# Order of the expert row gathers on GpSimd: four rows of U and four of V in turn, in place of one and one

## The reference

```python
def peer_ffn(h, w_q, sub_keys, u_tab, v_tab):
    q = (hf @ w_q).reshape(n_tok, PEER_HEADS, 2, PEER_HALF)
    half_scores = jnp.einsum('thpd,hpnd->thpn', q, sub_keys)
    s_top, i_top = lax.top_k(half_scores, PEER_TOPK)
    ...
    best, pos = lax.top_k(cand, PEER_TOPK)
    expert_idx = jnp.take_along_axis(cand_idx, pos, axis=-1)
    gates = jax.nn.softmax(best, axis=-1)
    def block(args):
        xb, ib, gb = args
        act = jnp.einsum('td,thkd->thk', xb, u_tab[ib])
        w = gb * jax.nn.gelu(act, approximate=False)
        return jnp.einsum('thk,thkd->td', w, v_tab[ib])
```

## Time and profile before

| | us |
|---|---|
| median of 3 runs | 2479.94 (2478.25 to 2479.95) |
| profiled execution, its own time | 2479.11 |
| its span, first to last instruction | 2477.4 |
| TensorE busy | 1984.5 (80%) |
| DVE busy | 1280.2 (52%) |
| GpSimd busy | 552.6 (22%) |
| ACT busy | 264.5 (11%) |
| moved by DMA | 793.18 MB, mean 320 GB/s |

### The profile page before, as it was taken

One profiled execution on the slowest core, in us unless ns is written; L12 is line 12 of the kernel. 1 busy time (PEld: TensorE's weight loads), 2 busy tenths in 40 slices (PEclk: granted clock), 3 DMA queues, 4 the chain that ended last, 5 costly groups with the idle time before them and its releaser, 6 DMA issues.

```text
span 2477.4 us, 19344 instructions
## 1 busy us (share of the span) xinstructions
PE 1984.5 (80%) x7000; PEld 1284.3 (52%) x7000; DVE 1280.2 (52%) x1633; ACT 264.5 (11%) x521; POOL 552.6 (22%) x551
## 2 busy tenths in 40 slices
PE   0399999998999999979677777777776777777777
PEld 0388888887888888868432222222222222222223
DVE  8634577775222122168865555565564444444443
ACT  0011112221000000020110101001011100010001
POOL 1000000000000000002454333334344333333341
PEclk9999999999999999999899999999998999999999
DMA  9868676553344336328899999999997999999996
GB/s 398 370 248 335 257 306 271 221 225 164 136 143 162 135 107 264 121 110 336 328 415 421 422 422 422 422 422 422 422 421 323 422 422 422 421 422 422 422 422 263
DMA packets 92379, 793.18 MB, mean 320 GB/s; under 512 B 10657, under 2 KB 10657, under 8 KB 11313
## 3 DMA queue, kind: packets, MB, share of 16 engines
q0 software_dynamic: 78512, 606.14, 59.0%
q1 hardware_dynamic: 13824, 186.55, 19.4%
q10 hardware_dynamic: 2, 0.02, 0.0%
HBM read 790.57 MB, written 2.10 MB: 320 GB/s over the span
## 4 chain that ended last, share of the span: by engine, by line
DMA 40%; PE 40%; DVE 13%; issue 4%; POOL 1%; ACT 1%; DVEq 0%; POOLq 0%; ACTq 0%; SPq 0%
DMA arena<-expert_u,expert 37%; PE ps L529 27%; PE ps L537 9%; DVE arena L1004 6%; DMA arena<-ada 2%; PE ps L690 2%; DMA arena<-expert_v,expert 1%; DVE mod_rows L731 1%; DVE buf_b L739 1%; POOL arena L361 1%; DVE work L827 1%; DVE work L824 1%; PE ps L545 1%; PE ps L644 0%; PE ps L677 0%
## 5 line engine op out<-in xcount | busy, mean ns | idle before, releaser
L690 PE MATMUL ps<-arena,work 128*128 128x512 f32 x1520 | 703.6, 608 | 254.1 <-DMA arena<-expert_v,expert 234.8
L1004 DVE CUSTOM_DVE_ANT_0 arena<-arena,buf_b 128x2048 f32<-128x2048 f32 x256 | 585.7, 2292 | 525.7 <-DMA arena<-expert_u,expert 524.6
L690 PEld LDWEIGHTS ps<-arena,work 128*128 128x128 f32 x1520 | 278.5, 192 | 678.1 <-issue 509.1
L361 POOL DMA_INDIRECT arena<-expert_u,expert x256 | 267.9, 1046 | 1220.2 <-DVE work L1004 695.3
L529 PE MATMUL ps<-buf_a,arena 128*128 128x256 f32 x2304 | 507.7, 382 | 10.9 <-DVE arena L845 5.2
L529 PEld LDWEIGHTS ps<-buf_a,arena 128*128 128x128 f32 x2304 | 440.8, 192 | 74.8 <-issue 14.7
L690 PE MATMUL ps<-mod_rows,work 128*128 128x512 f32 x504 | 230.6, 601 | 75.2 <-DMA mod_rows<-expert_v,expert 75.2
L529 PE MATMUL ps<-arena 128*128 128x256 f32 x1024 | 223.7, 379 | 1.0 <-ACT arena L471 1.0
L361 POOL DMA_INDIRECT arena<-expert_v,expert x192 | 194.6, 1013 | 84.7 <-issue 69.8
L529 PEld LDWEIGHTS ps<-arena 128*128 128x128 f32 x1024 | 193.9, 190 | 27.3 <-issue 1.3
L690 PEld LDWEIGHTS ps<-mod_rows,work 128*128 128x128 f32 x504 | 91.0, 190 | 214.3 <-issue 170.2
(11 more groups left out here) (192 smaller groups left out, 900.9 us busy)
## 6 DMA issues: line engine op xcount, KB each, us to landing
arena<-weights SPq DMA_DIRECT2D x68, 2048.0 KB, 8.2
arena<-ada POOLq DMA_DIRECT2D x32, 2048.0 KB, 11.8
arena<-ada SPq DMA_DIRECT2D x16, 2048.0 KB, 14.7
arena<-expert_u,expert POOLq DMA_INDIRECT x256
arena<-expert_v,expert POOLq DMA_INDIRECT x192, 18.0
buf_a<-x_t SPq DMA_DIRECT2D x1, 2048.0 KB, 20.9
arena<-ln_rows POOLq DMA_DIRECT2D x1, 2048.0 KB, 6.9
buf_a<-x_rows SPq DMA_DIRECT2D x1, 2048.0 KB, 7.9
```

The source lines that it names most:

```text
L361: pool.indirect_dma_start(slots[row % ring], None, table, bass.IndirectOffsetOnAxis(ap=expert[:, n // HEADS, column:column + 1], axis=0))\
L690: last = mm(ps[:, 4 * b + n, :], diag[:, s], v_slot[s][:, n * 512:(n + 1) * 512], start=first and e == 0, stop=False, skip_group_check=True)
L1004: v.tensor_tensor_reduce(out=u_slot[s], in0=u_slot[s], in1=h2[:, n // HEADS], scale=1.0, scalar=0.0, op0=ALU.mult, op1=ALU.add, accum_out= ...
```

## The change

Inside the turn of head n the 16 steps are cut into four groups of four (`U_RING` is 4). In each group GpSimd first issues U rows e = first to first + 3 of head n, then V rows first to first + 3 of head n - 1. In the turn n = 1 the first two groups have no V rows. What is issued, into which slots, and what is waited for before each gather stay the same; nothing on another engine is changed.

```diff
--- before.py
+++ after.py
@@ -379,10 +379,12 @@
                 gather_v(0, e)
             for n in range(1, BLOCKS * HEADS):
                 wait_alone(pool, s_ex, n + 1)
-                for e in range(TOPK):
-                    gather_u(n, e)
-                    if n > 1 or e >= V_RING:
-                        gather_v(n - 1, e)
+                for first in range(0, TOPK, U_RING):
+                    for e in range(first, first + U_RING):
+                        gather_u(n, e)
+                    for e in range(first, first + U_RING):
+                        if n > 1 or e >= V_RING:
+                            gather_v(n - 1, e)
             for e in range(TOPK):
                 gather_v(BLOCKS * HEADS - 1, e)
```

## The result

| | before | after |
|---|---|---|
| median of 5 runs | 2479.19 us | 2493.08 us |
| range | 2478.25 to 2479.95 | 2492.32 to 2493.97 |
| ratio to before | | 1.0056, 95% interval 1.0041 to 1.0071 |
| profiled execution, span | 2477.4 us | 2490.7 us |

The changed kernel is 13.9 us slower; 2494 was forecast. Lines of the kernel lie two further down (L1006 is the reduce, L692 the product with a V row, L464 and L465 the factor of the LayerNorm).

The account below looks back on a forecast made before the run. DMA was taken as the bound once row gathers run, except at the hole and the end; 7.8 (hole) + 5.4 (end) + 1.2 (first head) = 14.4 us, forecast 2494 us, 8 in 10 within 2486 to 2501.

Parts of the forecast that it names:

- The full stretch costs nothing: Stretch where the DMA queue is full: grouping adds nothing, since U slots have cover and PE isn't the bound over a cycle.
- the slots' cover of 11 us: U ring in the full stretch: about 11 us of slack per U row, against 5.5 us of possible delays.
- The rival in which the U ring runs dry: Rival B: delayed reduces and slower issues eat the cover in seven heads, adding 17 us, 2511; chance 0.08.
- the one in which PE becomes the bound: Rival C: clock at half for whole bursts, 7.7 us in each of 60 cycles, over 400 us; chance 0.01.
- rows of one table are read faster: Rival D: side by side reads in the lookup gain, so not slower, 2480 or somewhat below; chance 0.05.
- The clock falls in the gap: PE between bursts: each burst of four V rows begins at half clock, costing 2.5 us, between 1.7 and 3.1.
- The hole: Near 1890 us in head 9, DVE waits for ACT's rstd: +7.8 us from later burst end, cold start, missing transfer.
- The missing transfer: At the hole, V8 now comes after U11, which can't be issued; one transfer less runs, 2.5 us.
- covered, up to 1 us not: DVE chain ahead of the hole's wait: starts 5.3 us later, counted as covered, up to 1 us not.
- The end: PE's last run, heads 14 and 15: +5.4 us, 2.9 of backlog and 2.5 of cold clock.
- The first head: First head of this loop: queue runs empty while U10 waits for its slot, +1.2 us, bounds 0 and 2.5.
- The rival without the clock: Rival A: clock doesn't fall in the gaps or recovers before rows that count; 9.4 us slower, 2489; chance 0.22.

Follow-up runs that it names:

- e1: Groups of four only in turns 2 to 7 and 10 to 14, one and one in turns 1, 8, 9, 15; 2479.40 us against 2478.95 before.
- e2: Kernel before with groups of four in turns 8 and 9 alone, around the hole; 2486.56 us against 2478.95 before.
- e6: Changed kernel with steps 8 to 11 of turn 9 issued one and one, V row 8 queued before the hole; 2490.28 us against 2478.75 before.
- e5: Changed kernel with TensorE multiplying a zero matrix in gaps, so two bursts of each head begin at full clock; 2487.81 us against 2478.75 before.
- e9: Groups of two instead of four in every turn; 2486.43 us against 2479.41 before.
- e10: Kernel before, but V rows 12 to 15 of head 14 issued before U rows 12 to 15 of head 15; 2481.01 us against 2479.41 before.
- e4: Kernel before with groups of four in turn 1 alone; 2479.90 us against 2478.95 before.
- e3: Kernel before with one group of four, steps 12 to 15 of turn 15; 2485.02 us against 2478.95 before.
- e7: Kernel before with the last piece of block 0's output after reduce 10 of turn 9 instead of reduce 4; 2466.91 us against 2478.75 before.

## Why the prediction was right, point by point

**The full stretch costs nothing: right, shown by e1.** 44 groups, 0.5 us with an interval around zero. The longer issues of GpSimd (1622 ns in the mean) and the cold matmuls are there and cost nothing that the time shows; that the slots' cover of 11 us and PE's gap absorb them is the prediction's reading, and it fits. The rival in which the U ring runs dry falls, and the one in which PE becomes the bound too: e1 holds the groups at the same DMA rate (423 GB/s in its window). So does the one in which rows of one table are read faster: with four in a burst the reduces still start 2.49 us apart. One reading of the rows was off: GpSimd issues a U row 0.8 us after its slot's reduce ends (2394.99 against 2391.91 + 2.29), not 0.5 to 0.6. The cover was worked out from the issue on and stays 11 us.

**The clock falls in the gap: right in kind, and somewhat smaller where it counts.** The term was 2.5 us for each place, between 1.7 and 3.1. Measured in the changed kernel: 15.67 - 13.90 = 1.8 us in both. This is partly luck. Of the 57 groups that PE begins after 1262 us in that run, two were warm (14.00 us), and the other 54 before the last run took 15.4 to 17.0 us, 16.1 in the mean, which is 2.2 over a warm one. At the hole the group took 16.5 us in e2 and 16.6 in e6, 2.6 and 2.7 over. So 2.5 wasn't far from the usual cost, and the two groups that are waited for happened to be short ones. e5 shows that this part of the loss goes when the clock is kept up. The Trainium skill ("TensorE: Matmul & The Clock Gate", section "HAM oscillation — how this bites in real kernels") says that groups of matmuls between DMA waits start cold each time. The trace of the changed kernel agrees in 55 of 57 groups, behind idle times of 2.8 to 25.7 us; the one of e9 agrees in only 32 of 62, behind 2.7 to 2.9 us. What e1 adds is that in most places nobody pays for it.

**The hole, forecast +7.8, measured +8.2 in the changed kernel's piece, +9.5 in that of e2 and +7.6 by the median of e2.** The backlog of 2.8 us and the cold start of 1.8 are in the rows (ACT's last diagonal 5.1 us later, of which 0.4 is the later begin of head 9). The missing transfer is shown by e6 (2.3 us by its trace, 13.9 - 11.5 = 2.4 by the medians). These three are 7.1, and the stretch from head 9 to head 10 lost 7.7; the other 0.5 of the 8.2 lies in heads 10 to 14, within the scatter of that stretch. The 0.6 us left over has a candidate in the time that I had put at "covered, up to 1 us not": DVE's pieces run back to back before the wait, and U row 7 is issued at 1866.13 only. Windows of the changed kernel there (the last three columns are PEclk, DMA share and GB/s):

```profile
1860.00:1865.00 5.00, 5.00 (x13) 2.13 (x12) 4.93 (x9) 0.63 (x2) 0.94 (x1) 1.00 0.94 346
1865.00:1870.00 5.00, 5.00 (x13) 2.28 (x12) 5.00 (x6) 0.58 (x2) 3.26 (x3) 1.00 0.57 187
```

The DMA share is 0.57 from 1865 to 1870; in the kernel before it was full. In the changed kernel V row 4 of head 8, from which PE starts, still landed nearly when it should (1875.58, against 1845.44 + 12 x 2.485 = 1875.3), so here this dip explains 0.3 us at most. In e2 it is more:

```profile
1875.17 9.61 PE L693 MATMUL ps<-mod_rows,work 128*128 128x512 f32 x16 [4.26 <-DMA mod_rows<-expert_v,expert]
```

Head 9 began at 1844.14 there, so V row 4 was due at 1844.14 + 12 x 2.485 = 1874.0 and came 1.2 us late. With 2.8, 2.6 of clock and 2.5 for the missing transfer this makes 9.1 of the 9.4 us that e2 lost from head 9 to head 10. So what was counted as covered isn't always. No experiment separates this term, and the 0.3 left in both runs is of the size of the scatter.

**The end, forecast +5.4, measured +4.7.** 2.9 us of backlog (e5: 2.9 with a warm clock) and 1.8 us of clock in place of 2.5. e10 shows that it isn't the burst that costs but what is left of it when the last U row lands.

**The first head, forecast +1.2: not confirmed.** e4 gives 0.95 us by the medians with an interval around zero, and its piece 0.5. The step that failed is the zero that I set against 1.3 us: I wrote that V8 and V9 filled the queue there before. They also stood ahead of U9 and delayed it, and the windows say how little there was to lose. The kernel before (columns as above):

```profile
1235.00:1260.00 25.00, 22.62 (x53) 9.80 (x52) 17.62 (x29) 4.46 (x8) 20.85 (x14) 1.00 0.95 375
```

The changed kernel:

```profile
1235.00:1260.00 25.00, 18.39 (x38) 7.83 (x37) 20.30 (x34) 3.34 (x7) 18.27 (x13) 0.86 0.96 378
```

The share is 0.95 before and 0.96 after. The mechanism is there, in GpSimd's row of the changed kernel for U row 10 (through at 1243.4, where 1244.9 was forecast; this run is 1.1 us ahead there), but its cost isn't:

```profile
1241.20 2.24 POOL L361 DMA_INDIRECT arena<-expert_u,expert  x1 [3.10 <-DVE work L1006]
```

**The sum,** 14.4 us against 13.9, is nearer than its terms deserve, and that is luck: the clock's was too large by 1.4 us over both places in the profiled run and the first head's has no measured size, while the hole held about 1 us more. The parts run alone give by their medians 7.6 (e2) + 6.1 (e3) + 0.95 (e4) = 14.7 us, with 2 to 3 us of uncertainty in each, so the places are settled and the tenths are not. The rival without the clock would have been 9.4 us; e5, which is this case made real, gave 9.1.

**The hole itself** was only used in the prediction as the place where things wait. In the kernel before six heads of 32 transfers would take 6 x 32 x 2.485 = 477.1 us, and the piece takes 492.2, so some 15 us are lost in it, 14.3 of them in head 9 (93.81 against 32 x 2.485 = 79.5), where the hole is. e7 shows that it was the larger matter: moving one piece of DVE's work by six rows brings 11.8 us, while none of the orders of the gathers tried here brought anything.

## What to carry to other kernels

When a queue is full, as here, the order of what stands in it needn't cost or bring anything by itself (44 groups in e1: 0.5 us); look for the few consumers that wait for one particular entry, and count how many transfers stand before it and how long its engine still works on what landed with it. An engine that is slower per item than the transfers (3.45 against 2.485 us here) lives from the items in between that it doesn't process, so alternate them; where they must stand in a block at the end, the block goes first (1.6 us lost in e10, 6.1 in e3). And before changing an order, look at what makes the queue run empty at all: here it was one wait in DVE's program, which left the queue without a landing for 14.9 us.

## What the runs showed of the hardware that I had not expected

- The length of the gap alone doesn't tell whether the clock falls. In the pairs of e9 the same 2.7 to 2.9 us of idle were followed by a warm pair (7.1 us) 30 times and by a cold one (8.5 to 10.2 us) 32 times. In some stretches cold and warm alternate, for behind a cold pair the gap is only 1.1 us; in others several warm pairs follow one another.
- The DMA share falls before the last landing. In the changed kernel it was 0.57 from 1865 to 1870 us and the row awaited at 1875.58 still came on time. In the kernel before it was near zero while TensorE waited for V row 8, which it took at 1887.33. So when the queue ran dry is told by landings, not by the share alone. The windows of the kernel before, same columns:

```profile
1882.00:1884.00 2.00, 1.54 (x4) 0.86 (x5) 0.00 (x0) 0.00 (x0) 0.00 (x0) 1.00 0.22 90
1884.00:1886.00 2.00, 2.00 (x5) 0.58 (x4) 0.00 (x0) 0.00 (x0) 0.00 (x0) 1.00 0.06 25
```

- Stores of 1 MB that had run in the hole seem to cost 2.4 us once the hole was gone: the two reduces behind them come 1.2 us late each, at an unchanged 427 GB/s (e7).
